# Two-layer hybrid decoder kernel: half of each scan step's elementwise work goes from VectorE to ScalarE, and VectorE's part is cut in two

## The reference

```
a_cs  = cumsum(dtc * a_neg)                        # per head, within the chunk
decay = exp(where(causal, a_cs[l] - a_cs[s], -inf))
y_diag = (C B^T) * decay @ xdt                     # xdt = x * dt
states = (B * exp(a_cs[last] - a_cs))^T @ xdt
prev   = prev * exp(a_cs[last]) + states
y_off  = C @ prev * exp(a_cs)
```

## Time and profile before

| | |
|---|---|
| median of 3 runs | 1670.09 us (1669.96 to 1671.18) |
| profiled execution | 1675.85 us, its span 1674.1 us |
| busy: PE, DVE, ACT, POOL | 94%, 64%, 36%, 3% of the span |
| chain that ended last | PE 69%, DVE 19%, ACT 8%, issue 3%, DMA 1% |

### The profile page before, as it was taken

The page is one execution under the profiler, slowest core; times in us unless marked ns, Lnnn a source line. Parts: engine busy times, 40 slices in busy tenths (PEclk is TensorE's granted clock), DMA queues, the critical chain, the costliest instruction groups (busy, mean ns, idle before and its releaser), DMA issues.

```text
span 1674.1 us, 18545 instructions
## 1 busy us (share of the span) xinstructions
PE 1570.2 (94%) x7062; PEld 1248.1 (75%) x7062; DVE 1072.6 (64%) x1746; ACT 610.3 (36%) x847; POOL 44.6 (3%) x86
## 2 busy tenths in 40 slices
PE   6999989999989779999999999899999798799997
PEld 5877767777867667888877877677777686678886
DVE  7445674899999656533454467558999985573221
ACT  6444443344333234222244354433443332352220
POOL 0000000000000000101000000000000000001010
PEclk9999999999999889999999999899999898899999
DMA  5322222222322213445422222122113232125441
GB/s 209 100 85 89 76 88 63 65 74 64 95 75 99 85 51 104 134 144 151 142 85 85 80 97 88 63 70 69 64 63 104 83 104 70 57 83 167 141 151 63
DMA packets 44423, 158.13 MB, mean 94 GB/s; under 512 B 5520, under 2 KB 5808, under 8 KB 44336
## 3 DMA queue, kind: packets, MB, share of 16 engines
q1 hardware_dynamic: 36720, 129.64, 24.0%
q0 software_dynamic: 6464, 23.12, 4.9%
q10 hardware_dynamic: 1152, 4.19, 0.6%
HBM read 148.50 MB, written 8.44 MB: 94 GB/s over the span
## 4 chain that ended last, share of the span: by engine, by line
PE 69%; DVE 19%; ACT 8%; issue 3%; DMA 1%; DVEq 0%; SPq 0%; ACTq 0%; POOL 0%; POOLq 0%
PE acc L480 14%; PE acc L481 14%; PE acc L482 14%; PE S L480 3%; PE S L482 3%; PE S L481 3%; PE S L485 3%; DVE wlo L958 3%; ACT whi L731 3%; DVE xb L949 3%; DVE cacc L1006 3%; PE T L480 2%; PE T L482 2%; PE T L481 2%; ACT L719 1%
## 5 line engine op out<-in xcount | busy, mean ns | idle before, releaser
L480 PE MATMUL acc<-hhi,whi 128*128 128x512 f32 (+1 forms) x1504 | 610.4, 406 | 35.3 <-DVE wlo L958 35.3
L958 DVE TENSOR_TENSOR wlo<-stage,whi 128x1024 fp32r<-128x1024 f32 (+3 forms) x252 | 300.3, 1196 | 469.4 <-ACT whi L731 467.6
L481 PE MATMUL acc<-hlo,whi 128*128 128x512 f32 (+1 forms) x1504 | 595.0, 396 | 0.0
L482 PE MATMUL acc<-hhi,wlo 128*128 128x512 f32 (+1 forms) x1504 | 594.4, 395 | 0.0
L731 ACT ACTIVATE whi<-stage 128x1024 fp32r<-128x1024 f32 (+3 forms) x252 | 259.6, 1036 | 519.1 <-PE acc L482 302.4
L480 PEld LDWEIGHTS acc<-hhi,whi 128*128 128x128 f32 (+1 forms) x1504 | 287.2, 191 | 100.3 <-DVE wlo L958 36.9
L482 PEld LDWEIGHTS acc<-hhi,wlo 128*128 128x128 f32 (+1 forms) x1504 | 286.6, 191 | 64.2
L481 PEld LDWEIGHTS acc<-hlo,whi 128*128 128x128 f32 (+1 forms) x1504 | 287.3, 191 | 63.2 <-issue 3.9
L1006 DVE SCALAR_TENSOR_TENSOR cacc<-glu,pv,cacc 128x512 f32<-128x512 f32 x240 | 171.7, 748 | 4.6
L480 PE MATMUL S<-hhi,whi 128*128 128x512 f32 x192 | 75.5, 393 | 0.0
L482 PE MATMUL S<-hhi,wlo 128*128 128x512 f32 x192 | 74.7, 389 | 0.0
(11 more groups left out here) (226 smaller groups left out, 1599.5 us busy)
## 6 DMA issues: line engine op xcount, KB each, us to landing
stage<-weights SPq DMA_DIRECT2D x236, 512.0 KB, 3.4
y_features<-xg POOLq DMA_DIRECT2D x32, 256.0 KB, 4.1
acsb<-acs_rows POOLq DMA_DIRECT2D x16, 384.0 KB, 4.3
xg<-x_features ACTq DMA_DIRECT2D x8, 512.0 KB, 11.3
xr<-x_features POOLq DMA_DIRECT2D x16, 256.0 KB, 4.2
xr<-y_features POOLq DMA_DIRECT2D x16, 256.0 KB, 4.0
stage<-weights SPq DMA_DIRECT2D x8, 256.0 KB, 2.7
stage<-weights SPq DMA_DIRECT2D x4, 384.0 KB, 3.0
```

The costliest lines, as they stand in the source:

```text
L480: nc.tensor.matmul(out, a, c, start=start, stop=False)
L481: nc.tensor.matmul(out, a, d, start=False, stop=False)
L482: return nc.tensor.matmul(out, b, c, start=False, stop=stop)
L958: nc.vector.tensor_tensor(wlo[u % RING][:, 0:w], stage[u % STAGE][:, 0:w], whi[u % RING][:, 0:w].bitcast(F32), ALU.subtract).then_inc(lo_d ...
```

## The change

ScalarE's part of `ssd_a` now begins with six Relu activations that write relu(own - acsb) into `mt`; the later exponential has scale -1, so that it is the same exp(min(acsb - own, 0)). `cd` is made by an exponential of six columns of `acsb`, and `btok` by a copy from PSUM, both on ScalarE. VectorE's `ssd_a` keeps the argument of `dte` and one tap; the rest is a new task `ssd_c`, hung one step later, at u = 55 + 2s. There it stands behind the split of that step's unit and ahead of the tile's evacuation, which became a task of its own (`evac`). TensorE's, POOL's and SP's lists are as before.

```diff
     for s in range(8):
         put(54 + 2 * s, "ssd_a", s)
+        put(55 + 2 * s, "ssd_c", s)
         put(56 + 2 * s, "ssd_b", s)
...
-            for name, *args in hk.get(2 * j + half, []):
+            here = hk.get(2 * j + half, [])
+            s += [(name, tuple(args), []) for name, *args in here if name == "ssd_c"]
+            if half == 1:
+                s.append(("evac", (j,), []))
+            for name, *args in [task for task in here if task[0] != "ssd_c"]:
...
                         if s:
                             act.wait_ge(ssd_y.sem, ssd_y.at(layer, s))
+                        g, c = s // NT, s % NT
+                        for h in range(GH):
+                            one = acst[:, 12 * c + 6 * g + h:12 * c + 6 * g + h + 1]
+                            nc.scalar.activation(mt[:, h, :], acsb[:, h, :], ACT.Relu, scale=-1.0,
+                                                 bias=one).then_inc(seg_pos.sem, 1)
                         act.wait_ge(dte_in.sem, dte_in.at(layer, s + 1))
+                        a(None, cd, acsb[:, :, P - 1], ACT.Exp)
                         a(dte_exp, dte, dte, ACT.Exp)
                         a(ecs_exp, ecs[:, :, :], acsb[:, :, :], ACT.Exp)
-                        act.wait_ge(seg_in.sem, seg_in.at(layer, s + 1))
-                        a(seg_exp, mt[:, :, :], mt[:, :, :], ACT.Exp)
+                        act.wait_ge(ssd_turned.sem, ssd_turned.at(layer, s + 1))
+                        a(None, btok[:, :], T[0][:, 384:512], ACT.Copy)
+                        act.wait_ge(seg_pos.sem, seg_pos.at(layer, GH * (s + 1)))
+                        a(seg_exp, mt[:, :, :], mt[:, :, :], ACT.Exp, scale=-1.0)
...
-                        tt(dte_in, dte, acsb[:, :, P - 1], acst[:, own_t], ALU.subtract, go=True)
-                        for h in range(GH):
-                            one = acst[:, 12 * c + 6 * g + h:12 * c + 6 * g + h + 1]
-                            ts(seg_in if h == GH - 1 else None, mt[:, h, :], acsb[:, h, :], one, ALU.subtract, 0.0,
-                               ALU.min, go=True)
+                        tt(dte_in, dte, acsb[:, :, P - 1], acst[:, own_t], ALU.subtract)
                         convolve(1)
+                    elif name == "ssd_c":
...
                         dve.wait_ge(ssd_turned.sem, ssd_turned.at(layer, s + 1))
                         x3 = lambda ap: ap.rearrange("p (h q) -> p h q", h=GH)
-                        d(None, nc.vector.tensor_copy(btok[:, :], T[0][:, 384:512]), go=True)
...
                         dve.wait_ge(ecs_exp.sem, ecs_exp.at(layer, s + 1))
-                        d(None, nc.vector.tensor_copy(cd, ecs[:, :, P - 1]))
```

More of the change, by code:

```diff
@@ L378, in hybrid_kernel @@
         ecs_exp = sig("ecs_exp", 8)
-        seg_in = sig("seg_in", 8)
+        seg_pos = sig("seg_pos", 8 * GH)
         seg_exp = sig("seg_exp", 8)
@@ L397, in hybrid_kernel @@
                    acs_ready, acs48_ready, proj_taken, sq_part, sq_ready, head_r, qk_ready, max_ready, exp_done,
-                   rinv_ready, prob_ready, o_taken, xb_ready, dte_in, dte_exp, ecs_exp, seg_in, seg_exp, ssd_in,
+                   rinv_ready, prob_ready, o_taken, xb_ready, dte_in, dte_exp, ecs_exp, seg_exp, ssd_in,
                    ssd_taken, conv_sum_in, conv_r, pw_in, pw_hi, pw_lo, pw_taken, ssd_sq, ssd_r, branch_ready)
@@ L792, in _ @@
                             x_hi(k)
-                    if name == "in" and args[1] == 1:
+                    if name == "evac":
                         kind, i, _ = TILES[args[0]]
@@ L1230, in _ @@
                             dve.wait_ge(ssd_y.sem, ssd_y.at(layer, s))
-                        tt(dte_in, dte, acsb[:, :, P - 1], acst[:, own_t], ALU.subtract, go=True)
-                        for h in range(GH):
-                            one = acst[:, 12 * c + 6 * g + h:12 * c + 6 * g + h + 1]
-                            ts(seg_in if h == GH - 1 else None, mt[:, h, :], acsb[:, h, :], one, ALU.subtract, 0.0,
-                               ALU.min, go=True)
-                        convolve(1)
+                        tt(dte_in, dte, acsb[:, :, P - 1], acst[:, own_t], ALU.subtract)
+                        convolve(1)
+                    elif name == "ssd_c":
+                        s = args[0]
+                        g, c = s // NT, s % NT
+                        own_t = slice(12 * c + 6 * g, 12 * c + 6 * g + 6)
+                        b = slice(c * P, c * P + P)
                         dve.wait_ge(ssd_turned.sem, ssd_turned.at(layer, s + 1))
                         x3 = lambda ap: ap.rearrange("p (h q) -> p h q", h=GH)
-                        d(None, nc.vector.tensor_copy(btok[:, :], T[0][:, 384:512]), go=True)
                         tt(None, cbm[:, :], T[1][:, 0:P], until, ALU.mult, go=True)
```

## The result

| | time | ratio to before, 95% |
|---|---|---|
| before | 1670.63 us (median of 4, 1669.96 to 1674.75) | |
| after | 1691.19 us (median of 4, 1690.65 to 1691.40) | 1.0114 [1.0098, 1.0131] |
| forecast | 1693.7 us, range 1684 to 1701 | |

The account below looks back on a forecast made before the run. It took VectorE's round to bound the scan's first half and TensorE the second. Per layer 8.5 + 3.3 us, over two layers 23.6, on 1670.09 gave 1693.7 us, range 1684 to 1701.

Parts of the forecast that it names:

- The mechanism of the first half: Scan steps 0 to 3: VectorE's split waits for ScalarE's `whi`, evacuation 3.27 + 3 x 1.75 us later, 8.5 us a layer.
- The Relus: Six on ScalarE take 1.8 us (1.3 to 2.4), hidden in its idling from step 1 on, in line in step 0.
- The saved VectorE work counts: Faster rival: eight steps beside `xbc` save 1.5 us each, 12 us, giving 1658 us; chance 6%.
- The second half: Scan steps 4 to 7: TensorE's `ssd_b` of step 7 comes at 563.66 instead of 560.36, 3.3 us a layer.
- the ring: From step 4: products, POOL's load, Relus, exponentials, `whi`, `wlo`, products; 14.7 us a round against TensorE's 13.7.
- Step 4 met TensorE: Step 4's products end at 519.36, TensorE began `ssd_b` at 519.24 before: met with 0.1 to 0.3 us.
- The waits in steps 5 to 7: TensorE waits for the scan product `mt` about 1 to 1.5 us a step there.
- The rival on the clock: TensorE's clock falls in the second half too, up to 1.7 us each time; with slow Relus 1702 us; chance 13%.
- TensorE's waits in the first half: Waits for `mt` grow to 4 or 5 us a step, with 66 - 55 us to spare.
- Only the first half pays: Rival: load lands in 3.5 us, Relus take 1.3, TensorE takes up the second half's delays; 1687 us; chance 20%.

Follow-up runs that it names:

- split_only: Kernel before with only VectorE's `ssd_a` cut behind its tap, the products behind the next weight split, all work left on VectorE; 1692.05 us, ratio 1.0105.
- whi_first: Kernel after with ScalarE making `whi` ahead of the exponentials and `btok` right behind the Relus; 1665.3 us, ratio 0.9951.
- work_only: Kernel after with VectorE's products back in `ssd_a`, in front of the split, and `btok` right behind the Relus; 1664.29 us, ratio 0.9945.
- acsb_two: Kernel after with two buffers for `acsb`, so that POOL starts each load one step earlier; 1696.19 us, ratio 1.0128.
- relu_twice: Kernel after with each of the six Relus made twice; 1704.9 us, ratio 1.0177.
- after_again: Kernel after run once more with no edit; 1690.86 us, ratio 1.0114.
- btok_early: Kernel after with only ScalarE's copy `btok` moved right behind the Relus; 1691.97 us, ratio 1.0096.

## Why the prediction was right, and where it wasn't

**The mechanism of the first half was right, and its terms nearly so.** Split_only and whi_first show the mechanism from both sides: it is the lead of ScalarE's `whi` over VectorE's `wlo` that was spent. Forecast: VectorE's `wlo` waits 3.2 us (4.7 in step 0), the step takes 8.24 us (9.76). Measured: 2.89 (4.45), and 8.01 (9.57). A layer grows by 3.08 + 3 x 1.52 = 7.64 us instead of 8.5; the table has 69.70 - 62.06 = 7.64. The 0.23 us a step come from small terms: ScalarE starts 0.20 us behind VectorE and not 0.28; from `ecs` to `btok` it is 0.88 and not 0.92; from `mt` to `whi` and on to `wlo` 1.97 and not 2.04; `wlo` and the products take 4.17 and not 4.21.

**The Relus** take 1.87 us for six, forecast 1.8. The tile `acsb` of the kernel after lists them (minimum, median, maximum in ns):

```profile
L892 ACT ACTIVATE mt<-acsb,small x96: 383/387/404, 441.9 to 1394.4; 128x128 f32<-128x128 f32 x96
```

Each lasts 0.387 us but the next starts some 0.30 us after it, so six in a row cost less than six times one. The Trainium skill, "ScalarE: Activation LUTs", section "What ACT_TABLE_LOAD costs", gives about 280 ns and 0.833 ns a column for an activation with a pointer bias, which at 128 columns makes an estimate of 387 ns. The median in the trace agrees. The Trainium skill, "ScalarE: Activation LUTs", section "Rules for kernel authors", advises to give relu to VectorE. On the speed of the engines the traces agree: VectorE does a head in 0.20 us and ScalarE in 0.30. On the kernel's time the runs decide against the advice here: work_only, which moves the six heads and the two copies, is 9.3 us faster, because VectorE's list sets the pace and ScalarE idled 3 to 5 us at that point.

**"The saved VectorE work counts"**, the faster rival, stated a true value in the wrong place. Its condition, that the whole chain be done within 0.8 us, does not hold in this change; where the products stand in front of the split, the work is hidden and the saving comes through.

**The second half: the size came out right, the ring was wrong.** Forecast 3.3 us a layer, from a round of 14.7 us through POOL's load. Measured: T to S7 grew by 3.8 us in layer 0 and 2.5 in layer 1, of which 2.4 and 2.1 lie in the rounds from S4 to S7 and the rest in T to S4. Step 4 met TensorE as said: no wait at 526.30. But acsb_two shows that the load's round had slack, and that VectorE's own round of 14.88 us carries the delay from step 4 into step 5 and 6. My step "from there a ring closes" took the right products and `whi` chain and closed them through the wrong link. One of its terms was off: the load landed in 3.6 us (median), not 4.3. With that landing my own sum gives a round of 14.0 us and 1.2 us a layer, so the agreement in size is luck: a round that I had not reckoned happens to be as long as the one that I had, and a term that I had left out (below) made up the rest. What the same ring forecast for relu_twice came true because there, with twelve Relus in it, the load's round does overtake VectorE's. The waits in steps 5 to 7 were said to be 1 to 1.5 us each; they are 1.60, 0.53 and 0. The loads themselves in the kernel after:

```profile
DMA to landing us min/median/max: 3.4/3.6/4.7
```

**A term I left out: TensorE's clock around step 4.** Windows of equal length behind the `xb` wait, kernel after and then before, columns as in the earlier trace rows:

```profile
511.50:517.50 6.00, 5.92 (x17) 4.95 (x18) 4.28 (x9) 3.96 (x12) 0.00 (x0) 0.50 0.28 87
```

```profile
505.90:511.90 6.00, 5.99 (x23) 4.93 (x23) 5.54 (x16) 2.16 (x4) 0.00 (x0) 0.72 0.28 87
```

After two waits 4.42 and 2.46 us long TensorE has a granted clock of 0.50, the level of 1.2 GHz, for the whole 6 us; before, 0.72. The difference of 0.22 over 6 us is 1.3 us at full clock, and T to S4 is 1.4 us longer in layer 0. In layer 1 the same windows have 0.57 and 0.63, 0.4 us at full clock, and T to S4 is 0.4 us longer. The rival on the clock had this price (up to 1.7 us) but set it in steps 5 to 7 behind a wait for `mt`; it came ahead of step 4 behind the wait for `xb`. In after_again it is +1.1 and +0.4, in btok_early +0.1 and -0.4: real in some executions. The lengths of the two waits don't decide it by themselves: split_only has 4.38 and 2.47 us there, nearly the same, and a granted clock of 0.72 in the 6 us behind them. What does is open.

**TensorE's waits in the first half** were forecast at 4 to 5 us; steps 0 and 3 have 3.93 and 4.42, but steps 1 and 2 only 2.92 and 2.80. That was of no account for the time, since the pace there was VectorE's.

"Only the first half pays" (1687) is refuted by S4 to S7, 2.4 and 2.1 us longer. One half of its condition nearly came true, the load in 3.6 us, but the Relus take 1.87 us and not 1.3, and VectorE's round holds TensorE up whatever the load does.

## What to carry to other kernels

Before work goes to an idle engine, look at what is queued behind it there, and who waits for that: an idle engine's lead over its reader is a reserve, and it is spent before the idle time is. Where a change does two things, run each alone: here the total of +21 us hid a half worth -9. And a resource that is idle while its input isn't there offers no time; the Relus were free in steps 1 to 3 and cost their full length in step 0.

## What the runs showed that I had not expected

A Relu is 0.387 us long in the trace, and six follow each other at some 0.30 us. The spacing was forecast, from the earlier trace rows; that a single one is a quarter longer than its share of the row was not. Two rounds that look equally tight (14.7 us forecast through the load, 14.9 measured on VectorE) were told apart by cutting one of them: a wait named "DMA" in the trace of after (1.75 us in step 5) was worth nothing. And the time from the `xb` wait to step 4 varies between executions of the same kernel by 0.3 us, and by up to 1.3 between nearly equal ones, with the clock granted behind the wait.
